# Output products of two feed-forwards: from eight products of quarters to seven

## What is computed

```python
# block 2: gated, 1024 -> 2 x 2816 -> 1024
h = rmsnorm(x, pre_ffn_g);  u, v = split(h @ w_ffn_in_2);  hid = silu(u) * v        # 512 x 2816
x = x + rmsnorm(hid @ w_ffn_out_2, post_ffn_g)                                     # ffout2
# block 3: squared relu, 1024 -> 4096 -> 1024
h = rmsnorm(x, norm_mlp_pre);  hid = relu(h @ w_ff1_3) ** 2                        # 512 x 4096
out = x + rmsnorm(hid @ w_ff2_3, norm_mlp_post)                                    # ff2_3
```

## Time and profile before

| | |
|---|---|
| median of 3 runs | 3370.14 us |
| span of the profiled execution | 3367.3 us |
| TensorE busy | 3271.0 us, 97% |
| VectorE busy | 1153.8 us, 34% |
| ScalarE busy | 573.5 us, 17% |
| stretch of `ffout2` (2186.22 to 2338.26) | 152.04 us |
| stretch of `ff2_3` up to its second mean (3134.28 to 3355.04) | 220.76 us |

### The profile page before, as it was taken

The page is one execution under the profiler, slowest core; times in us unless marked ns, Lnnn a source line. Parts: engine busy times, 40 slices in busy tenths (PEclk is TensorE's granted clock), DMA queues, the critical chain, the costliest instruction groups (busy, mean ns, idle before and its releaser), DMA issues.

```text
span 3367.3 us, 34075 instructions
## 1 busy us (share of the span) xinstructions
PE 3271.0 (97%) x13966; PEld 1842.7 (55%) x13966; DVE 1153.8 (34%) x2254; ACT 573.5 (17%) x1184; POOL 1.4 (0%) x6
## 2 busy tenths in 40 slices
PE   8999989999999999999999999999999999999998
PEld 5555553344333433377885588846444444588545
DVE  2046531111111111166653454402260992264101
ACT  2033220110010001123223310002231002210001
POOL 0000000000000000000000000000000000000000
PEclk9999989999999999999988999999999999999999
DMA  5122349999999999920000222222202222222220
GB/s 243 51 100 86 116 175 408 428 429 428 429 429 428 429 428 429 429 82 21 26 1 19 82 80 96 78 79 97 75 25 75 75 75 75 75 76 87 89 75 25
DMA packets 42799, 585.20 MB, mean 174 GB/s; under 512 B 4736, under 2 KB 6784, under 8 KB 7232
## 3 DMA queue, kind: packets, MB, share of 16 engines
q1 hardware_dynamic: 42464, 582.45, 42.5%
q0 software_dynamic: 224, 1.18, 0.1%
HBM read 581.51 MB, written 2.10 MB: 173 GB/s over the span
## 4 chain that ended last, share of the span: by engine, by line
PE 87%; DMA 8%; DVE 2%; ACT 1%; issue 1%; SPq 0%; DVEq 0%; ACTq 0%
PE PS L243 23%; PE PS L410 15%; PE PS L1252 11%; DMA ring<-in_weights 8%; PE PS L1232 4%; PE PS L635 3%; PE PS L839 3%; PE PS L321 3%; PE PS L1186 2%; PE PS L2139 2%; PE PS L295 2%; PE PS L351 2%; PE PS L1219 1%; PE PS L1168 1%; PE PS L641 1%; PE PS L1742 1%
## 5 line engine op out<-in xcount | busy, mean ns | idle before, releaser
L243 PE MATMUL PS<-A,ring 128*128 128x512 f32 x1244 | 536.5, 593 | 0.7 <-ACT A L1783 0.7
L243 PEld LDWEIGHTS PS<-A,ring 128*128 128x128 f32 x1244 | 236.0, 190 | 298.5 <-issue 297.1
L1252 PE MATMUL PS<-A 128*64 128x512 f32 x1280 | 293.9, 601 | 2.3 <-DMA A<-in_weights 0.6
L243 PE MATMUL PS<-H,ring 128*128 128x512 f32 x544 | 234.3, 592 | 0.0
L410 PE MATMUL PS<-A 128*128 128x256 f32 x1032 | 230.2, 379 | 0.0
L410 PEld LDWEIGHTS PS<-A 128*128 128x128 f32 x1032 | 195.9, 190 | 27.7 <-issue 0.8
L1232 PE MATMUL PS<-ring,A 128*64 128x512 f32 x768 | 173.0, 597 | 16.8 <-DMA ring<-in_weights 16.6
L1324 DVE TENSOR_TENSOR A<-A,PS 64x512 f32<-64x512 f32 x64 | 44.1, 690 | 420.9 <-ACT A L1281 420.9
L1252 PEld LDWEIGHTS PS<-A 128*64 128x64 f32 x1280 | 85.1, 137 | 177.5 <-issue 169.4
L1252 PE MATMUL PS<-ring,A 128*64 128x512 f32 x768 | 175.4, 599 | 0.8 <-DMA ring<-in_weights 0.3
L243 PEld LDWEIGHTS PS<-H,ring 128*128 128x128 f32 x544 | 103.4, 190 | 129.7 <-issue 129.6
(11 more groups left out here) (493 smaller groups left out, 3866.5 us busy)
## 6 DMA issues: line engine op xcount, KB each, us to landing
ring<-in_weights SPq DMA_DIRECT2D x178, 2048.0 KB, 14.0
A<-in_weights SPq DMA_DIRECT2D x96, 2048.0 KB, 24.0
X<-in_x SPq DMA_DIRECT2D x1, 2048.0 KB, 12.9
vec<-in_vec SPq DMA_DIRECT2D x1, 1047.0 KB, 10.9
A<-in_ctx SPq DMA_DIRECT2D x1, 1024.0 KB, 19.0
out_y<-X SPq DMA_DIRECT2D x2, 512.0 KB, 2.9
out_y<-X SPq DMA_DIRECT2D x4, 256.0 KB, 2.3
con<-in_const SPq DMA_DIRECT2D x1, 972.0 KB, 12.8
```

The lines of the kernel that those rows point to most:

```text
L243: mm = nc.tensor.matmul(bank[:, 0:out_width], weight_tile(name, n), moving(k), start=k == 0, stop=k == k_tiles - 1)
L1252: mm = nc.tensor.matmul(PS[CAP * up:CAP * (up + 1), c % 2, :], XS[:, k, CAP * b:CAP * (b + 1)], w[:, n:n + 4, :].rearrange("p a b -> p (a ...
```

## The change

`ffout2` and `ff2_3` are made as pairs of output tiles, each with seven quarter products. The sum is 22 or 32 tiles deep; it is cut into blocks of eight tiles (the last of `ffout2` is six), and the seven products run over all blocks, each in a PSUM bank of its own that stays open from the first block to the last. VectorE makes the input sums `T2` to `T4` anew for every pair and block, beside `S1` to `S4`. `T1` overwrites the second half of the tokens of one half block, once.

```diff
-    ("ffout2", 8, NFF2, 7),
+    ("ffout2", 24, WT // 4, 0),
...
-    ("ff2_3", 8, 32, 7),
+    ("ff2_3", 8, 32, 0),
...
+def deep_blocks(k_tiles):
+    return [(k, min(4, (k_tiles - k) // 2)) for k in range(0, k_tiles, 8)]
...
+        DEEP_BANK = {P1_: 0, P2_: 3, P6_: 1, P7_: 6, P4_: 2, P5_: 4, P3_: 7}
...
+        def deep_products(pe, name):
+            def product(p, prod, b, w, x):
+                n = d["blocks"][b][1]
+                for k in range(n):
+                    mm = nc.tensor.matmul(PS[:, DEEP_BANK[prod], 0:TC], w[:, k, :], x[:, k, :], start=b == k == 0,
+                                          stop=b == nb - 1 and k == n - 1)
+                    if k == 0 and ended[0]:
+                        mm.then_inc(S["chunk_used"], 1)
+                        ended[0] = False
+                mm.then_inc(S["deep_made"], 1)
...
+            for p in range(4):
+                for b in range(nb):
+                    if p == 0:
+                        pe.wait_ge(S[d["signal"]], d["blocks"][b][0] + 2 * d["blocks"][b][1])
+                    chunk_loaded(pe, CHUNK0[name] + places[p, b][0])
...
+                    product(p, P1_, b, A11, deep_input(name, b, 0, 0))
...
+                    product(p, P2_, b, A12, deep_input(name, b, 1, 0))
+                if p == 0:
+                    pe.wait_ge(S["c21"], end)
+                else:
+                    pe.wait_ge(S["deep_out"], deep_out(name, p - 1, "c12"))
+                for b in range(nb):
+                    pe.wait_ge(S["deep_summed"], deep_summed(name, p, "S2", b))
+                    product(p, P6_, b, S2, deep_turned(name, p, "T2", b)[0])
+                    pe.wait_ge(S["deep_summed"], deep_summed(name, p, "S3", b))
+                    product(p, P7_, b, S3, deep_turned(name, p, "T3", b)[0])
+                    pe.wait_ge(S["deep_summed"], deep_summed(name, p, "T4", b))
+                    product(p, P4_, b, A22, deep_turned(name, p, "T4", b)[0])
+                    if p < 3:
+                        product(p, P5_, b, S1, deep_input(name, b, 0, 1))
+                        product(p, P3_, b, S4, deep_input(name, b, 1, 1))
+                    ended[0] = released(p, b)
+            for b in range(nb):
+                product(3, P5_, b, deep_set(name, 3, b)[0], deep_input(name, b, 0, 1))
+                if b == 0:
+                    deep_mean(pe, name, 0)
+            for b in range(nb):
+                product(3, P3_, b, deep_set(name, 3, b)[3], deep_input(name, b, 1, 1))
...
+        def deep_dve(dve, name, gain):
+            def sums(p, b):
+                if p == 0:
+                    tt(x(0, 1), x(0, 1), x(0, 0), ALU.subtract).then_inc(S["deep_summed"], 1)
+                turned_free("T2")
+                tt(T2, x(1, 1), x(0, 1), ALU.subtract).then_inc(S["deep_summed"], 1)
+                if p == 3 and b >= 2:
+                    dve.wait_ge(S["deep_made"], deep_made(name, 2, P3_, nb - 1))
+                elif q >= 2:
+                    dve.wait_ge(S["deep_made"], deep_made(name, (q - 2) // nb, P3_, (q - 2) % nb))
+                tt(S1, A21, A22, ALU.add).then_inc(S["deep_summed"], 1)
+                tt(S2, S1, A11, ALU.subtract).then_inc(S["deep_summed"], 1)
+                turned_free("T3")
+                tt(T3, T2, x(0, 0), ALU.subtract).then_inc(S["deep_summed"], 1)
+                tt(S3, A11, A21, ALU.subtract).then_inc(S["deep_summed"], 1)
+                tt(S4, A12, S2, ALU.subtract).then_inc(S["deep_summed"], 1)
+                turned_free("T4")
+                tt(T4, x(1, 0), T2, ALU.subtract).then_inc(S["deep_summed"], 1)
...
+            for p in range(4):
+                sums(p, 0)
+                if p:
+                    outs(p - 1)
+                sums(p, 1)
+                first_out(p)
+                if p:
+                    for f in (2 * p - 2, 2 * p - 1):
+                        if f:
+                            add_square(f)
+                for b in range(2, nb):
+                    sums(p, b)
+            for h, sq in ((0, 7), (1, 9)):
+                if h == 0:
+                    outs_to_c21(3)
+                dve.wait_ge(S["deep_sq"], 10 * d["n"] + sq)
+                dve.wait_ge(S["deep_acc"], 7 * d["n"] + 5)
+                tt(acc[:, half_of(h)], acc[:, half_of(h)], d["sq"][1][:, half_of(h)], ALU.add).then_inc(S["deep_acc"], 1)
+                if h == 0:
+                    outs_to_q(3)
+                else:
+                    out(3, "c12", H[:, 6, TC:], P3_, u2, "q")
+                    dve.wait_ge(S["deep_out"], deep_out(name, 3, "c12"))
+                scaled_added_dve(dve, h, gain)
...
+        def deep_norm_act(act, name, gain=None, raw=None):
+            deep_act(act, name)
+            nc.scalar.preload_act_table(ACT.Ln)
+            deep_last_act(act, name, "c21")
+            half_power_act(act, 0)
+            deep_last_act(act, name, "c22")
+            if gain:
+                pre_norm_half(act, 0, range(8), gain, raw)
+            nc.scalar.preload_act_table(ACT.Ln)
+            deep_last_act(act, name, "c12")
+            half_power_act(act, 1)
...
```

More of the change, by code:

```diff
@@ new lines, in deep_summed, with deep_out @@
+        def deep_summed(name, p, what, b):
+            nb = len(DEEP[name]["blocks"])
+            before = sum(4 * 7 * len(d["blocks"]) + len(d["blocks"]) for d in DEEP.values() if d["n"] < DEEP[name]["n"])
+            at = ("T2", "S1", "S2", "T3", "S3", "S4", "T4").index(what) + 1
+            return before + (8 * b + 1 if p == 0 else 8 * nb + 7 * (nb * (p - 1) + b)) + at
+        def deep_out(name, p, part):
+            return 28 * DEEP[name]["n"] + 7 * p + ("c11", "u2", "u3", "c21", "c22", "q", "c12").index(part) + 1
@@ new lines, in deep_weights, with deep_set, deep_turned @@
+        def deep_weights(name, p, b):
+            chunk, at = DEEP[name]["places"][p, b]
+            n = DEEP[name]["blocks"][b][1]
+            v = slot_view(slot_use(CHUNK0[name] + chunk)[0])
+            return [v[:, at + j * n:at + (j + 1) * n, :] for j in range(4)]
+        def deep_set(name, p, b):
+            nb = len(DEEP[name]["blocks"])
+            q = nb * p + b
+            return DEEP[name]["sums"][b if p == 3 and b >= 2 else (q if p < 3 else nb * p + b) % 2]
+        def deep_turned(name, p, what, b):
+            seq = 3 * (len(DEEP[name]["blocks"]) * p + b) + DEEP_TURNED[what]
+            return DEEP[name]["turned"][seq % 4][:, 0:DEEP[name]["blocks"][b][1], :], seq
@@ new lines, in deep_mean @@
+        def deep_mean(pe, name, h):
+            d = DEEP[name]
+            acc, _, last = d["sq"]
+            if h == 0:
+                pe.wait_ge(S["deep_out"], deep_out(name, 3, "c21"))
+            pe.wait_ge(S["deep_acc"], 7 * d["n"] + 6 + h)
+            nc.tensor.matmul(PS[:, 5 + h, half_of(h)], mean, acc[:, half_of(h)], start=True, stop=False)
+            pe.wait_ge(S["deep_sq"], 10 * d["n"] + 8 + 2 * h)
+            nc.tensor.matmul(PS[:, 5 + h, half_of(h)], mean, last[:, half_of(h)], start=False, stop=True
+                             ).then_inc(S["mean"], 1)
@@ L518, in link, with deep_last_act @@
+        def deep_last_act(act, name, part):
+            act.wait_ge(S["deep_out"], deep_out(name, 3, part))
+            tile, buffer, h = {"c21": (7, 2, 0), "c22": (7, 1, 1), "c12": (6, 2, 1)}[part]
+            nc.scalar.activation(DEEP[name]["sq"][buffer][:, half_of(h)], H[:, tile, half_of(h)], ACT.Square
+                                 ).then_inc(S["deep_sq"], 1)
         def link(eng, engine, ins):
@@ L2469, in third_tensor @@
         def third_tensor(pe):
[L2470 removed]
+            first_products_by_halves(pe, "win3a", RAW, lambda: deep_mean(pe, "ffout2", 1))
             moving = normed_input(pe)
@@ L2734, in tiles_fk, with deep_weights_laid @@
     return w.reshape(k // P, P, f // P, P).transpose(1, 2, 0, 3).reshape(P, -1)
+def deep_weights_laid(w):
+    k, f = w.shape
+    tiles = w.reshape(k // P, P, f // P, P).transpose(1, 2, 0, 3)
+    places = deep_places(k // P)
+    out = np.zeros((max(c for c, _ in places.values()) + 1, P, WT, P), w.dtype)
+    for (p, b), (chunk, at) in places.items():
+        k0, n = deep_blocks(k // P)[b]
+        out[chunk, :, at:at + 4 * n] = tiles[:, 2 * p:2 * p + 2, k0:k0 + 2 * n].reshape(P, 4 * n, P)
+    return out.reshape(-1, P, WT * P)
 def chunks(*laid):
```

245 lines of the change are left out of this document (193 added, 52 removed).

## The result

The changed kernel took 3330.68 us (median of 4 runs, 3324.77 to 3338.92) against 3369.73 before (4 runs, 3369.07 to 3377.58): 0.988 of the time, 95% interval 0.986 to 0.990. Two later sets of the same kernel gave 3327.94 and 3327.39; all 12 runs together have their median at 3328.1, the 41 runs of the kernel before that were made beside them at 3371.5. So 43 us were gained, and 42.9 forecast. The profiled execution spans 3327.2 us, for 3324.4 forecast.

The account below looks back on a forecast made before the run. TensorE's matmul time was taken to bound both stages. Terms 44.7 - 0.1 - 1.2 - 0.5 = 42.9 us took the span from 3367.3 to 3324.4; 2.8 more gave 3327.2 us, 80% range 3323 to 3340.

Parts of the forecast that it names:

- Matmuls removed and added, 44.7 us: In `ffout2` and `ff2_3`, matmuls removed (151.2 and 219.9 us) less those added (133.0 and 193.4): 44.7 us gained.
- VectorE's sums hidden, one place without cover: VectorE's sums in both stages stay hidden, except at the last block of `ff2_3`'s last pair: 0.1 us.
- unseen sizes: Six-tile block's sums of 768 and 384, absent from the trace: taken as 0.88 and 0.48 us, middles of bounds.
- Tails, 1.2 and 0.5 us: At the second mean, PE waits 1.2 us in `ffout2`; in `ff2_3` that matmul starts 0.5 us later.
- Weights: Weight chunks held longer stay hidden: landing 7.7 us, tightest gap 22.0 us in `ffout2`, 14 us of slack.
- Semaphores and banks: Merged semaphores and another starting bank cost 0; 0.4 to 1.2 us if a reader waited for one further event.
- PE waits on VectorE: Rivals: more waits at P6 and tails, 13 us, 3340, 12%; sums exposed block by block, +123, 3493, 3%.
- on DMA: Rival: weights late, 14 releases each followed by a 24.0 us landing against 22.0, 28 us: 3355, chance 2%.
- not 0.491: Rival: PE's time stays because quarter matmuls take 0.491 us, a seventh more: 3370, chance 1%.
- The loads stay beside matmuls: Rival: weight loads come into the open, 540 added records costing 103 us: 3428, slower, chance 2%.
- about half: VectorE's load in the two changed stages: about half busy.
- The term of 2.8 us from span to median: The median of the runs lies 2.8 us above the profiled span: 3324.4 becomes 3327.2 us.

Follow-up runs that it names:

- Experiment 1: The changed kernel run again unaltered, twice: 3327.94 and 3327.39 us.
- experiment 2: Changed kernel with `ffout2` put back to the code of the kernel before, seven products in `ff2_3` alone: 3346.25 us.
- Experiments 3 and 4: Changed kernel with every input sum `T2` to `T4` computed twice: 3349.74 us; then with `S1` waiting one block back in the first three pairs: 3355.24 us.
- experiment 5: Changed kernel with `c12` and its sum of squares amid VectorE's scaling, ScalarE's square before its last two raw tiles, in `ffout2`: 3341.78 us, again 3334.50.
- reordered kernel: The kernel of experiment 5, also called the reordered tail, against the changed kernel: 3337.7 us over both sets (11 runs).
- two reorderings: The reordered kernel, 3337.7 us, and the same with the last pair's sums of squares moved later, 3337.85 us.
- the sums of squares later: Reordered kernel with the last pair's two sums of squares moved behind the sums of blocks 2 and 3: 3337.85 us.
- before + 2: Kernel before with two spare matmuls (0.9 us) behind the second mean of `ffout2`: 3381.76 us, against 3371.5 without.

## Why the prediction was right

- *Matmuls removed and added, 44.7 us.* Right to 0.2 us a stage. Experiment 1 shows both lengths three times over, experiment 2 that the stages' gains add up. The quarter matmul from the neighbouring stage, 0.4317 us, held for all.
- *VectorE's sums hidden, one place without cover.* Right, the place included: the only sum that PE waited for is `S2` of the last block of `ff2_3`, 0.25 us for 0.1. Experiments 3 and 4 moved the cost and the wait, and PE's waits came where the stepping of the two queues had put them, within 0.5 us in 22 and 2.5 in 25. The unseen sizes were 0.95 us for 768 elements and 0.55 for 384, starts 0.87 and 0.47 apart: the middles of the bounds.
- *Tails, 1.2 and 0.5 us.* 1.17 and 0.59. In `ffout2` the cause was as put, ScalarE's raw tiles and table load ahead of its square, all of it later because `c22` and `q` go ahead of the scaling; experiment 5 takes the wait away. In `ff2_3` the steps lie where the stepping had them (scaling from M + 6.05, `c12` until M + 12.7, the second mean matmul at M + 13.2), but no experiment touches them.
- *Weights.* 7.7 us to landing after too, never waited for. *Semaphores and banks*: no wait of PE between the two stages differs from before by as much as 0.1 us, but for the one at the second mean.
- *The rivals.* PE waits on VectorE 0.25 us and on DMA not at all in the two stages, and the quarter matmul takes 0.4317 us, not 0.491. The loads stay beside matmuls: 1512 records of 190 ns, with stationary operands in `A` and in the ring, in stretches of which PE's busy time fills the whole length. By the rule in the Trainium skill, "TensorE: Matmul & The Clock Gate", section "The mechanism", that the prediction used, they would have stood in the open; the measurement decides against it. The same section also lets a load go ahead into a background weight buffer, which the prediction left out; no run here tells whether these do.
- *What was off without harm.* VectorE is 65 to 68% busy in the stages, not about half. PE's busy time is 3230.9 us, not 3226, nearly all of the excess ahead of `ffout2`. The term of 2.8 us from span to median was the median of three runs less the span of one; a run's time lies 1.7 to 2.0 us above its own span, so some 1 us of it was scatter.
- *What the prediction lacked.* A term for the clock outside the two stages: the sum leaves the rest of the span as it was. The median of the first four runs was 3.5 us above the forecast; the profiled run was 1.7 above, with its span 2.8 above and `ffout2` starting 2.9 late. It could have been more: with the tail of `ffout2` 1.2 us shorter, the reordered kernel's median is 3337.7, 34 us under before in place of 43, and with 2.2 us of spare work behind the changed tail it is 3342.8. The range (3323 to 3340) held the first and not the second, and what width it had was there for waits and the scatter of a median. That the gain came out as large as forecast is in this part luck.

No kernel here beats the changed one. The two reorderings do what they should inside their stages (1.2 us in `ffout2`, 0.3 in `ff2_3`), and lose more than that in block 3.

## What to carry to other kernels

When a trade moves work from a full engine to one with room, price it by stepping the two queues against each other with the starts of neighbouring rows, and look at the last round, where the full engine has less to do per step: the mean load of an engine (65 to 68% busy here) says nothing of it. Check a gain in the stage's own window, and only then in the median: here a kernel that was a microsecond shorter ahead of block 3 had a median 10 us longer. Before calling a small edit worse, look for a stretch at a lower granted clock elsewhere, and add a microsecond of spare work next to the edit, to it and to the kernel without it, with ten runs or more of each side by side.

## What the runs showed that I had not expected

In block 3, at the passage from dense products to the attention's short matmuls, with one idle microsecond before the first of them, TensorE's clock was granted at 2.4 GHz throughout in some runs and fell to 1.2 GHz in others of the same kernel: 25 us at a mean of 0.56 in one profile, worth 11 us there (25 x 0.44), while `win3a` to `ff1_3` differs by 14.5 us between the reordered tail's two profiles. Four of the thirteen profiles show it (the reordered tail's first, the sums of squares later, the input sums twice, before + 2); the changed kernel's three don't. With two spare matmuls (0.9 us) 120 us earlier in the kernel before, 9 of 12 runs were in the upper group, against 3 of 17 without them on the same chip. What the clock's fall hangs on, the runs don't show.
